# Second block: who normalises the probabilities, and how queries and keys are rotated

## The reference

```
h    = rms_norm_2(x, gain)
proj = h @ w_in            # q, k, v, g of three branches, index q, index k, index w, forget, merge
oa = moba_attention(rope_partial(qa), rope_partial(ka), va) * silu(ga)
ob = dsa_attention(rope_partial(qb), rope_partial(kb), vb, rope_partial(q_idx), rope_partial(k_idx), w_idx) * silu(gb)
oc = forgetting_attention(qc, kc, vc, log_f) * silu(gc)
y  = [oa, ob, oc] @ w_branch;  merged = sum(sigmoid(merge_logit) * y);  x = x + merged @ w_out
```

## Time and profile before

| | |
|---|---|
| median of 3 runs | 1212.73 us (1211.58 to 1213.41) |
| the profiled execution | 1208.57 us, span 1206.8 us |
| PE busy | 1121.3 us, 93% of the span |
| DVE busy | 819.4 us, 68% |
| ACT busy | 645.7 us, 54% |
| second block, layer 0 / layer 1 | from about 530 / 872 us of the span on |
| chain that ended last | PE 77%, DVE 12%, ACT 5% |

### The profile page before, as it was taken

One profiled execution on the slowest core, in us unless ns is written; L12 is line 12 of the kernel. 1 busy time (PEld: TensorE's weight loads), 2 busy tenths in 40 slices (PEclk: granted clock), 3 DMA queues, 4 the chain that ended last, 5 costly groups with the idle time before them and its releaser, 6 DMA issues.

```text
span 1206.8 us, 20978 instructions
## 1 busy us (share of the span) xinstructions
PE 1121.3 (93%) x8007; PEld 991.1 (82%) x8007; DVE 819.4 (68%) x1803; ACT 645.7 (54%) x1260; POOL 2.4 (0%) x9
## 2 busy tenths in 40 slices
PE   4699999999888999779999999999799999999997
PEld 3477777767766778679899999999798999999996
DVE  3866766766656565579967886656589767766664
ACT  5665644567337644435555664444355656654443
POOL 0000000000000000000000000000000000000000
PEclk9899999999889999979999999999799999999999
DMA  7876654111322322415454556666345545566662
GB/s 240 247 235 203 186 177 117 53 53 53 88 61 62 114 70 83 122 47 140 124 149 117 148 157 183 187 181 175 88 124 139 141 124 139 150 182 181 186 175 70
DMA packets 277163, 165.07 MB, mean 137 GB/s; under 512 B 7092, under 2 KB 275112, under 8 KB 277064
## 3 DMA queue, kind: packets, MB, share of 16 engines
q1 hardware_dynamic: 276872, 163.08, 47.5%
q0 software_dynamic: 192, 0.66, 0.2%
HBM read 162.66 MB, written 1.05 MB: 136 GB/s over the span
## 4 chain that ended last, share of the span: by engine, by line
PE 77%; DVE 12%; ACT 5%; issue 4%; DMA 1%; SPq 0%; DVEq 0%; ACTq 0%
PE pj L1696 20%; PE pj L1697 19%; PE pj L1698 19%; PE pj L1764 3%; DVE w_lo L1134 2%; ACT w_hi L704 2%; PE tr L2096 1%; PE ac L1944 1%; PE sc L1932 1%; PE tr L1842 1%; DVE ntmp L1196 1%; PE sc L1835 1%; PE ac L2050 1%; DVE h_lo L1206 1%; DMA raw<-in_ada_w_dram 1%
## 5 line engine op out<-in xcount | busy, mean ns | idle before, releaser
L1696 PE MATMUL pj<-h_hi,w_hi 128*128 128x256 f32 (+1 forms) x1664 | 510.6, 307 | 9.1 <-DVE h_lo L1206 9.0
L1697 PE MATMUL pj<-h_lo,w_hi 128*128 128x256 f32 (+1 forms) x1664 | 498.7, 300 | 0.0
L1698 PE MATMUL pj<-h_hi,w_lo 128*128 128x256 f32 (+1 forms) x1664 | 498.6, 300 | 0.0
L1134 DVE TENSOR_TENSOR w_lo<-raw,w_hi 128x1024 fp32r<-128x1024 f32 (+1 forms) x258 | 309.6, 1202 | 151.9 <-ACT w_hi L704 150.9
L1696 PEld LDWEIGHTS pj<-h_hi,w_hi 128*128 128x128 f32 x1664 | 319.6, 192 | 36.0 <-issue 18.4
L1698 PEld LDWEIGHTS pj<-h_hi,w_lo 128*128 128x128 f32 x1664 | 319.7, 192 | 10.1
L1697 PEld LDWEIGHTS pj<-h_lo,w_hi 128*128 128x128 f32 x1664 | 320.1, 192 | 9.3 <-issue 1.2
L704 ACT ACTIVATE w_hi<-raw 128x1024 fp32r<-128x1024 f32 (+1 forms) x258 | 267.6, 1039 | 43.9 <-PE pj L1698 38.3
L1696 PE MATMUL pj<-m_hi,w_hi 128*128 128x256 f32 (+1 forms) x352 | 110.9, 315 | 13.4 <-DVE w_lo L1134 9.2
L1697 PE MATMUL pj<-m_lo,w_hi 128*128 128x256 f32 (+1 forms) x352 | 109.4, 311 | 0.0
L1698 PE MATMUL pj<-m_hi,w_lo 128*128 128x256 f32 (+1 forms) x352 | 109.2, 310 | 0.0
(11 more groups left out here) (270 smaller groups left out, 1320.1 us busy)
## 6 DMA issues: line engine op xcount, KB each, us to landing
raw<-in_w_in_dram SPq DMA_DIRECT2D x152, 512.0 KB, 3.8
raw<-in_ada_w_dram SPq DMA_DIRECT2D x48, 512.0 KB, 5.1
raw<-in_even_w_in_dram SPq DMA_DIRECT2D x28, 512.0 KB, 5.1
raw<-in_w_branch_dram SPq DMA_DIRECT2D x24, 512.0 KB, 3.5
raw<-in_w_out_dram SPq DMA_DIRECT2D x16, 512.0 KB, 4.3
raw<-in_odd_w_in_dram SPq DMA_DIRECT2D x11, 512.0 KB, 3.9
raw<-in_even_w_out_dram SPq DMA_DIRECT2D x8, 512.0 KB, 3.8
raw<-in_odd_w_out_dram SPq DMA_DIRECT2D x8, 512.0 KB, 3.8
```

The costliest lines, as they stand in the source:

```text
L1134: last = nc.vector.tensor_tensor(lo, src, hi.bitcast(F32), ALU.subtract)
L1696: nc.tensor.matmul(dst, lh, rh, start=first, stop=False)
L1697: nc.tensor.matmul(dst, lh, rl, start=False, stop=False)
L1698: return nc.tensor.matmul(dst, ll, rh, start=False, stop=final)
```

## The change

ScalarE now does the multiplications of the normalisation, after the four exponentials of the pair slot; VectorE is left with the two reciprocals, both at the end of the slot, behind `split_lo`. The rotation of a query chunk no longer happens when it is evacuated: query and key of a pair (or two index-query chunks) are written to the two halves of `rope` and rotated by one set of four operations over 2x256 columns, when the second of them is there. The rotation's first product is now made in place, and the shuffle comes first.

```diff
-ROPES1, ROPES2 = 2 * B_HEADS + 1 + 4, 1 + 4 + 2 * 8
+ROPES1, ROPES2 = 2 * B_HEADS + 1 + 4, 1 + 2 + 8
+def rope_number(pair):
+    return 3 + sum(BRANCH_ORDER[p // 4] != FORGET for p in range(pair))
+        qk_h = work[:, 0:2048].rearrange("p (a r n) -> p r a n", a=2, r=NQK)
@@ ScalarE, evacuation
-                            h_rope_input(1 + i, 1.0, src)
+                            h_rope_input(1 + i // 2, i % 2, 1.0, src)
-                                h_rope_input(h_rope_index(kind, i), scale, src)
+                                h_rope_input(rope_number(i), kind == "k", scale, src)
-                    act.wait_ge(rope_out, ROPES1 + lay * ROPES2 + max(i - 1, 0))
-                    nc.scalar.activation(rope[:, i % 2, :], src, ACT.Copy, scale=scale).then_inc(freed["act"], 1)
+                    act.wait_ge(rope_out, ROPES1 + lay * ROPES2 + n)
+                    nc.scalar.activation(rope[:, int(place), :], src, ACT.Copy, scale=scale).then_inc(freed["act"], 1)
@@ ScalarE, behind the exponentials of a pair slot
+                        for u in (2 * t, 2 * t + 1):
+                            act.wait_ge(recip_set, lay * 24 + u + 1)
+                            for i, (a, b) in enumerate(((0, 128), (128, 384))):
+                                j = 16 + 2 * (u % 4) + i
+                                nc.scalar.activation(expd[:, u % 2, a:b], expd[:, u % 2, a:b], ACT.Copy, scale=small[:, j:j + 1])\
+                                    .then_inc(prob2_set, 1)
@@ VectorE
+            def rotate_two(src, dst, cos, sin, shuffle):
+                dve.wait_ge(rope_out, rotations[0])
+                rotations[0] += 1
+                cos2, sin2 = (table.rearrange("p (a n) -> p a n", a=1).broadcast_to([P, 2, SEQ]) for table in (cos, sin))
+                after(nc.vector.stream_shuffle(terms2[:, :, :], src, shuffle))
+                nc.vector.tensor_tensor(src, src, cos2, ALU.mult)
+                after(nc.vector.tensor_tensor(terms2[:, :, :], terms2[:, :, :], sin2, ALU.mult))
+                nc.vector.tensor_tensor(dst, src, terms2[:, :, :], ALU.add).then_inc(rope_out, 1)
-                        if kind == "qi":
-                            h_rotate(1 + i, g, qi_h[:, i, :])
-                        elif kind in ("q", "k") and BRANCH_ORDER[i // 4] != FORGET:
-                            h_rotate(h_rope_index(kind, i), g, (q_h if kind == "q" else k_h)[:, i % NQK, :])
+                        if kind == "qi" and i % 2 == 1:
+                            dve.wait_ge(*freed_at(g, lay))
+                            rotate_two(rope[:, :, :], qi_h[:, i - 1:i + 1, :], pr_cos, pr_sin, PR_SHUFFLE)
+                        elif kind == "k" and BRANCH_ORDER[i // 4] != FORGET:
+                            dve.wait_ge(*freed_at(g, lay))
+                            rotate_two(rope[:, :, :], qk_h[:, i % NQK, :, :], pr_cos, pr_sin, PR_SHUFFLE)
-                def head_normalise(u):
+                def head_reciprocal(u):
                     j = 2 * (u % 4)
                     dve.wait_ge(exp2_set, lay * 48 + 2 * u + 2)
-                    after(nc.vector.reciprocal(small[:, 16 + j:18 + j], small[:, 8 + j:10 + j]))
-                    for i, (a, b) in enumerate(tile_cols):
-                        nc.vector.tensor_scalar(expd[:, u % 2, a:b], expd[:, u % 2, a:b], small[:, 16 + j + i:17 + j + i], None,
-                                                ALU.mult).then_inc(prob2_set, 1)
+                    nc.vector.reciprocal(small[:, 16 + j:18 + j], small[:, 8 + j:10 + j]).then_inc(recip_set, 1)
@@ VectorE, the loop over slots
-                    if s - 1 in PAIR_SLOT:
-                        head_normalise(2 * PAIR_SLOT[s - 1] + 1)
-                    if t is not None:
-                        head_normalise(2 * t)
                     if s < B2_IN:
                         split_lo(pos(s, lay) + AHEAD)
+                    if t is not None:
+                        head_reciprocal(2 * t)
+                        head_reciprocal(2 * t + 1)
@@ TensorE, index_scores and pair_scores
-                    pe.wait_ge(rope_out, ROPES1 + lay * ROPES2 + m + 2)
+                    pe.wait_ge(rope_out, ROPES1 + lay * ROPES2 + 2 + m // 2)
-                        pe.wait_ge(rope_out, ROPES1 + lay * ROPES2 + h_rope_index("k", pair) + 1)
+                        pe.wait_ge(rope_out, ROPES1 + lay * ROPES2 + rope_number(pair) + 1)
```

More of the change, by code:

```diff
@@ L238 @@
 MERGE_SLOT = {B2_CHUNKS.index(("branch", (2, mp))) + 2: [2 * mp, 2 * mp + 1] for mp in range(4)}
-ROPES1, ROPES2 = 2 * B_HEADS + 1 + 4, 1 + 4 + 2 * 8
-def h_rope_index(kind, pair):
-    before = sum(BRANCH_ORDER[p // 4] != FORGET for p in range(pair))
-    return 5 + 2 * before + (kind == "k")
+ROPES1, ROPES2 = 2 * B_HEADS + 1 + 4, 1 + 2 + 8
+def rope_number(pair):
+    return 3 + sum(BRANCH_ORDER[p // 4] != FORGET for p in range(pair))
 def gate_slot(b, m):
@@ L512, in build_program @@
             sem("sc2_done"), sem("neg_set"), sem("exp2_set"), sem("prob2_set"), sem("pv2_done"), sem("o2_set"))
+        recip_set = sem("recip_set")
         og_set, g_hi_set, g_lo_set = sem("og_set"), sem("g_hi_set"), sem("g_lo_set")
@@ L1023, in h_evacuate, with h_rope_input @@
                                 .then_inc(freed["act"], 1)
-                def h_rope_input(i, scale, src):
-                    act.wait_ge(rope_out, ROPES1 + lay * ROPES2 + max(i - 1, 0))
-                    nc.scalar.activation(rope[:, i % 2, :], src, ACT.Copy, scale=scale).then_inc(freed["act"], 1)
+                def h_rope_input(n, place, scale, src):
+                    act.wait_ge(rope_out, ROPES1 + lay * ROPES2 + n)
+                    nc.scalar.activation(rope[:, int(place), :], src, ACT.Copy, scale=scale).then_inc(freed["act"], 1)
                 def h_turned(use):
@@ L1509, in _ @@
                 masks = (mask[:, P:SEQ], mask)
[L1511 to L1516, removed]
                 def h_evacuate(c):
@@ L1612, in _ @@
                                                        sc[:, 0, 0:SEQ], ALU.mult, ALU.mult).then_inc(x_set, 1)
-                h_rotate(0, None, ki_h)
+                dve.wait_ge(misc_set, 2 * lay + 1)
+                rotate(rope[:, 0, :], ki_h, pr_cos, pr_sin, PR_SHUFFLE)
                 for s in range(B2_IN + B2_DRAIN):
```

## The result

| | before | after |
|---|---|---|
| median, 20 runs each on one chip | 1212.27 us (1207.96 to 1218.10) | 1215.55 us (1212.27 to 1218.81) |
| ratio after / before | | 1.0027, 95% interval 1.0015 to 1.0038 |
| the profiled execution | 1208.57 us, span 1206.8 us | 1215.99 us, span 1214.2 us |

The change makes the kernel 3.3 us slower, with an interval of 1.8 to 4.6 us. The page after shows what moved between the engines: DVE is rid of 34 us, ACT has 33 us more, and PE is still the engine that is nearly always busy.

The account below looks back on a forecast made before the run. TensorE bounds the second block nearly everywhere; followed slot by slot, each layer ends its busy stretch 1.42 us later, 2 x 1.42 = 2.8 us, so the median is 1212.73 + 2.8 = 1215.5 us; range 1208.3 to 1218.5.

Parts of the forecast that it names:

- The joint rotation at 2.70: VectorE's four operations on 2x256 columns take 2.70 us instead of 3.26 for two single rotations, saving 0.56 per rotated pair.
- ACT's multiplications at 1.39 a pair: ScalarE's scaled copies, 495 and 400 ns for 256 and 128 columns, take 0.69 us a unit, 1.39 a pair.
- Slot 3, 0.45: First index scores wait for index query 0, now rotated with query 1 in slot 2; TensorE late by about 0.45 us.
- Slots 11 and 12: VectorE idles 3.3 us, but for two reciprocals, until ScalarE has multiplied and evacuated k; slot 12's rotation starts at 576.88.
- Slots 14 and 15: VectorE waits 1.8 us for ScalarE, rotating at 591.19; TensorE's second three transposes come at about 591.0, so slot 15's stall stays.
- Slot 18: New TensorE wait for ScalarE's multiplication; next projection at 605.61 instead of 604.19, ending this stretch 1.42 us later.
- After slot 20: Search over, VectorE idles between slots and TensorE sets the pace, so the lateness is neither made up nor increased.
- Relief: Rival: ScalarE's round trip hides behind other VectorE work, the stall goes, 2 x -3.6 = -7.2 us, 1205.5; chance 0.14.
- the first fall: In the kernel before, TensorE's clock drops after the gap behind 588.07; the projection behind ran 1.14 us over its time.
- the clock rival: Rival: slot 18's new wait makes TensorE's clock fall a second time, 1.1 us a layer on top, 1217.8; chance 0.10.

Follow-up runs that it names:

- evacuation first: Changed kernel with ScalarE's multiplications moved to the following slot, behind the k chunk's evacuation; 1208.41 us, 0.9975 of the kernel before.
- the rotation alone: Changed kernel with VectorE's multiplications put back, leaving only the joint rotation; 1215.50 us, 1.0031 of the kernel before.
- two other orders: Changed kernel with ScalarE multiplying behind the k chunk's evacuation, 1208.41 us; or with VectorE's two reciprocals ahead of `split_lo`, 1210.23 us.
- one constant: Kernel before with TOPK_SLOT 21 instead of 12, so the search's first round moves from slot 12 to slot 21; 1204.74 us, ratio 0.9945.

## Why the prediction was right, step by step

The forecast was 1215.5 us by +1.42 us a layer; it came to 1215.55 by +1.49 and +1.70. That the two medians agree within 0.1 us is partly luck: the loss was forecast at 2.8 us and measured at 3.3, and the base, a median of 3 runs, lay 0.46 us above that of the 20. What the traces confirm is the way there.

- *The joint rotation at 2.70.* 581.92 to 584.63 is 2.71. Its distances are 0.77, 0.61, 0.72 and 0.61 against the 0.75, 0.61, 0.73 and 0.62 taken. The rule of the Trainium skill (VectorE: DVE Perf Modes, "The DRAIN you can't avoid"), that a semaphore between two Vector operations costs nothing, isn't borne out here: the two distances with a wait are 0.11 and 0.16 longer than the ones without (0.05 of the 0.16 is that the shuffle itself takes 0.74 for the 0.69 of the others), and the set would have cost 2.45 by it.
- *ACT's multiplications at 1.39 a pair.* 580.12 to 581.51, and again 594.44 to 595.83: 1.39 both times. The forms read 498 and 396 ns where 495 and 400 were taken:

```profile
L1106 ACT ACTIVATE expd<-expd,small 128x256 f32<-128x256 f32 x48 | 23.9, 498 | 0.0
...
L1106 ACT ACTIVATE expd<-expd,small 128x128 f32<-128x128 f32 x48 | 19.0, 396 | 13.0 <-DVE small L1606 13.0
```

- *Slot 3, 0.45.* The wait is 0.43 us and the slot starts 0.50 later; it stays so up to slot 14.
- *Slots 11 and 12.* Idle before the rotation forecast at 3.3 us, measured 578.61 to 581.92, 3.31. The rotation was forecast for 576.88; less the 4.98 it came at 576.94.
- *Slots 14 and 15.* Idle forecast at 1.8 behind the reciprocals, which is 2.04 from the end of `split_lo` (589.15 to 591.19), the way slot 12 is counted; measured 2.01 (594.23 to 596.24). The rotation was forecast for 591.19, it came at 591.26; PE's second three transposes for 591.0, they came at 591.09, against 591.01 before. So the stall's end stayed where it was, as forecast, while its start moved back with the schedule.
- *Slot 18.* A new wait for ACT; the next projection forecast for 605.61 came at 605.68. This small remainder is the whole of layer 0's 0.07. Layer 1 is 0.21 more because the kernel before lost 0.17 less there (68.40 against 68.57).
- *After slot 20.* No gain and no loss, as the 47.90 and 47.89 show.

Relief was to win if DVE idled less than 4.1 us between slot 11 and slot 18; it idled 3.31 + 2.01 = 5.3, and where less of it stands in the way (evacuation first) the relief does win, by 3.3 us. The clock didn't fall a second time in the kernel after, though layer 1 stalled for 1.78 us in slot 18. Nor would the first fall have mattered: behind slot 15 the granted clock is below full level in layer 0 and at full level in layer 1, and yet slot 19 starts at 70.06 and 70.10. Windows after, 20 us around slot 15 of both layers, columns as in the earlier trace rows:

```profile
585.00:605.00 20.00, 18.15 (x138) 15.87 (x137) 17.50 (x52) 10.32 (x27) 0.00 (x0) 0.91 0.39 106
925.00:945.00 20.00, 17.68 (x145) 15.33 (x145) 17.47 (x51) 11.63 (x29) 0.00 (x0) 1.00 0.31 83
```

PE reached slot 17 0.98 us earlier in layer 1, worked on at full level, and waited 1.48 us longer, in slot 17 (0.45 us for `w_lo`, a wait that I had not listed) and slot 18 (1.78 for 0.75): the end is set by the chain through DVE and ACT, and TensorE's clock inside it is slack. That I gave the clock rival 1.1 us a layer on top holds only behind slot 18, where the chain has let go; that is where the rotation alone lost 1.5.

What the prediction weighed too little is the rotation. It names the joint set as 0.56 us saved a pair; by itself it makes slot 12 1.1 us later on DVE, since the single rotation of q was free filler in a wait, and brings TensorE's slot 19 half a microsecond back in each layer. The kernel with it alone has a median 3.8 us up, of which the slots explain 1.1. The sum was right because the slots were followed one by one, and the idle time came out of the dependences rather than out of a saving.

## What to carry to other kernels

An engine that is late but has waits in its queue is not relieved by less work, if that work filled the waits: follow the queue instruction by instruction and ask what each one stands beside. When work is moved to another engine, its place in that queue and the place of what it waits for are worth more than its length; here the same instructions in two other orders were 6.5 and 4.7 us faster (-3.3 and -1.5 against the kernel before, for +3.3). And where one engine is overloaded for eight slots out of dozens, look first for what can leave those slots: one constant gave 7.2 us where the change, meant for the same place, lost 3.3.

## What the runs showed of the hardware that I had not expected

- The same stall of TensorE (0.39 and 1.27 us with three transposes between) was followed by a lower granted clock in one of six profiled layers, at a cost of 1.5 us, and not in the other five. In the kernel after, the stall of slot 15 (1.68 or 1.69, and 0.17 us) was followed by one in layer 0 and not in layer 1. Whether the clock falls behind such a stall can't be told from a single profile.
- The first block is untouched in all kernels, and yet the second block's slot 1 starts anywhere in a band of 6.2 us (535.38 to 541.62) from one profiled execution to the next. Comparing the two spans would have made the change's loss more than twice its size.
